# Residual stream with tokens on partitions: norms on one number per token, and tiles turned on TensorE, in a two-layer hybrid decoder step

## What is computed

```python
def rms_norm(x, g):
    y = x * rsqrt(mean(x * x, axis=-1) + EPS)
    return y * g
...
for l in range(2):
    h = rms_norm(x, norm_mix_pre[l])
    m = even_mixer(h) if l == 0 else odd_mixer(h)      # gating MLP + short conv | retention
    x = x + rms_norm(m, norm_mix_post[l])
    h = rms_norm(x, norm_x_pre[l])
    x = x + rms_norm(cross_attn(l, h, mem_k[l], mem_v[l]), norm_x_post[l])
    h = rms_norm(x, norm_ffn_pre[l])
    x = x + rms_norm(ffn(l, h), norm_ffn_post[l])
```

## Time and profile before

| | |
|---|---|
| median of 3 runs | 1286.12 us (1285.82 to 1286.32) |
| the profiled execution | 1280.77 us, of it the span 1278.7 us |
| PE busy | 1176.1 us (92% of the span) |
| DVE busy | 766.4 us (60%) |
| ACT busy | 584.6 us (46%) |
| POOL busy | 296.8 us (23%) |
| mean clock granted to PE | 0.974 of full |
| read from and written to HBM | 233.6 MB, 182 GB/s |

### The profile page before, as it was taken

How to read it: one execution, slowest core, us unless ns; L and a number is a source line. 1 busy time by engine, 2 the same in 40 slices (tenths; PEclk the granted TensorE clock), 3 DMA queues, 4 the chain that set the end, 5 groups by cost and what they waited for, 6 DMA issues and landing times.

```text
span 1278.7 us, 22925 instructions
## 1 busy us (share of the span) xinstructions
PE 1176.1 (92%) x8557; PEld 1085.2 (85%) x8557; DVE 766.4 (60%) x1020; ACT 584.6 (46%) x940; POOL 296.8 (23%) x521
## 2 busy tenths in 40 slices
PE   6999999997999999799999888899999979999995
PEld 4999898696999999699999333798986869999994
DVE  3685835427888743676555677457345278888343
ACT  5446543435666544523345221256334356665432
POOL 5001201114555620200000111004002135646202
PEclk9999999998999999899999899899999989999998
DMA  9748475832545445445444799847848325554531
GB/s 210 233 130 280 152 257 166 301 105 67 180 160 167 133 149 185 156 132 166 156 140 138 254 366 359 279 157 274 278 145 293 128 73 165 164 164 126 170 112 37
DMA packets 177267, 233.64 MB, mean 183 GB/s; under 512 B 5374, under 2 KB 153226, under 8 KB 177200
## 3 DMA queue, kind: packets, MB, share of 16 engines
q1 hardware_dynamic: 159088, 169.09, 40.8%
q0 software_dynamic: 18112, 63.60, 14.5%
HBM read 207.50 MB, written 25.16 MB: 182 GB/s over the span
## 4 chain that ended last, share of the span: by engine, by line
PE 83%; DVE 9%; ACT 5%; issue 2%; DMA 0%; POOL 0%; SPq 0%; ACTq 0%; DVEq 0%
PE ps L392 68%; PE ps L556 5%; ACT wh L324 2%; DVE xT L472 2%; DVE wl L327 2%; PE ps L1207 1%; PE ps L1308 1%; PE ps L1343 1%; PE ps L1319 1%; DVE rstd L433 1%; PE ps L1241 1%; PE ps L1219 1%; DVE raw L962 1%; PE ps L1292 1%; DVE hl L450 1%
## 5 line engine op out<-in xcount | busy, mean ns | idle before, releaser
L327 DVE TENSOR_TENSOR wl<-raw,wh 128x2048 fp32r<-128x2048 f32 (+2 forms) x154 | 331.7, 2154 | 309.6 <-ACT wh L324 309.5
L392 PE MATMUL ps<-hh,wh 128*128 128x288 f32 x1600 | 483.9, 302 | 34.8 <-DVE hl L450 28.2
L392 PE MATMUL ps<-hl,wh 128*128 128x288 f32 x1600 | 476.6, 298 | 0.0
L392 PE MATMUL ps<-hh,wl 128*128 128x288 f32 x1600 | 475.0, 297 | 0.0
L324 ACT ACTIVATE wh<-raw 128x2048 fp32r<-128x2048 f32 (+3 forms) x154 | 277.7, 1803 | 293.8 <-PE ps L392 292.8
L392 PEld LDWEIGHTS ps<-hh,wh 128*128 128x128 f32 x1600 | 304.1, 190 | 41.5 <-issue 33.7
L392 PEld LDWEIGHTS ps<-hh,wl 128*128 128x128 f32 x1600 | 305.7, 191 | 0.0
L392 PEld LDWEIGHTS ps<-hl,wh 128*128 128x128 f32 x1600 | 305.2, 191 | 0.3
L392 PE MATMUL ps<-aH,wh 128*128 128x288 f32 x352 | 104.2, 296 | 0.0
L392 PE MATMUL ps<-aL,wh 128*128 128x288 f32 x352 | 103.9, 295 | 0.0
L392 PE MATMUL ps<-aH,wl 128*128 128x288 f32 x352 | 103.6, 294 | 0.0
(11 more groups left out here) (296 smaller groups left out, 1642.1 us busy)
## 6 DMA issues: line engine op xcount, KB each, us to landing
raw<-w_ffn_up SPq DMA_DIRECT2D x44, 1024.0 KB, 5.1
raw<-w_in_odd SPq DMA_DIRECT2D x24, 1024.0 KB, 5.2
raw<-state_retention SPq DMA_DIRECT2D x16, 1024.0 KB, 7.4
out<-raw POOLq DMA_DIRECT2D x16, 1024.0 KB, 7.8
ring<-cache_mem_k POOLq DMA_DIRECT2D x14, 1024.0 KB, 5.6
raw<-w_ffn_down SPq DMA_DIRECT2D x16, 768.0 KB, 4.4
raw<-w_in_even SPq DMA_DIRECT2D x10, 1024.0 KB, 6.0
raw<-w_ffn_down SPq DMA_DIRECT2D x16, 640.0 KB, 4.1
```

Source lines behind the costliest of these rows:

```text
L327: e.tensor_tensor(wl[:, c % 2, 0:kn, :], src, wh[:, c % 2, 0:kn, :].bitcast(F32), ALU.subtract).then_inc(lo_ready, 1)
L392: mm = pe.matmul(out, lhsT, rhs, start=(kc == 0 and n_k == 0 and n == 0), stop=(kc == g.nk - 1 and n_k == kn - 1 and n == 2))
```

## The change

The stream is kept as `xn`: three groups of 128 tokens on partitions (tokens 0 to 127, 128 to 255, and 160 to 287, so that the third is full; `TOK`) by 1024 features. There a token's norm is one number on its partition.

- **Behind a branch**: ACT copies output tiles to `mT` already times the gain (DVE takes the last tile). `sums` leaves three tiles of squares; `ssq` uses the squares as weights against one column of ones, three token groups each, so that the sum is three columns of 128 tokens. `root_out` and `invert_out` work on 128 x 3. A throw-away root of one number loads ACT's table earlier. `turn_out` turns the four feature tiles of each half and token group to token rows (24 transposes), and `add_piece` on DVE adds them times the token's number into `xn`, in nine pieces of 256, 256 and 512 columns (`SPANS`) by three groups. POOL's `scale_branch` is gone.
- **Before a branch**: `turn_in` turns `xn` back, three transposes for each of eight feature tiles; `high_in` and `low_in` take `hh` and `hl` straight from PSUM. The squares are taken on ACT from `xn` by rows with an accumulated sum (`row_squares`), root and reciprocal are of 128 x 3, and `invert_in` and `spread` bring 1/root back to the transposed layout: a diagonal matrix for each group, multiplied with ones.
- **Where**: at the three direct places (`xo` to `up` twice, `down` to `in_odd`) as one sequence (`joint_act`, `joint_dve`, `joint_tokens`, a new `first_step`), whose second chunk begins with the passes that need only the high half (`late`). Under `xk` and `xv` the turns are hooks after single chunks. The transposes of old conv tails move from behind `xo` to between its chunks.
- **Start and end**: `xn` is loaded as it is (96 prompt rows twice) and stored by SP from `xn` at the end; `xT`, `yn` and their copies are gone.

The diff, cut:

```diff
-        def invert(dve, n):
-            dve.wait_ge(root_ready, n + 1)
-            dve.reciprocal(rstd[:], root[:]).then_inc(rstd_ready, 1)
...
+        def sums(dve, q):
+            dve.wait_ge(sq_ready, CREDIT + 8 * q + 4)
+            dve.tensor_tensor(sq[:, 0:2, :], sq[:, 0:2, :], sq[:, 2:4, :], ALU.add).then_inc(sum_step, 1)
...
+            dve.tensor_tensor(sq[:, 0, :], sq[:, 0, :], sq[:, 1, :], ALU.add).then_inc(sum_step, 1)
+
+        def ssq(pe, q):
+            pe.wait_ge(sum_step, 3 * q + 3)
+            for t in (0, 6, 7):
+                pe.wait_ge(sq_ready, CREDIT + 8 * q + t + 1)
+                for g in range(3):
+                    mm = pe.matmul(ps[:, 7, g:g + 1], sq[:, t, TOK[g]:TOK[g] + P], ones[:, 0:1], start=t == 0 and g == 0, stop=t == 7,
+                                   skip_group_check=True)
...
+        def root_out(act, q):
+            act.wait_ge(ssq_ready, q + 1)
+            act.activation(root_out_col, ps[:, 7, 0:3], ACT.Sqrt, bias=eps_col, scale=1.0 / D).then_inc(root_ready, 1)
...
+        def add_piece(dve, q, n):
+            span, g = divmod(n, 3)
+            c0, c1 = SPANS[span]
+            half = c0 // 512
+            dve.wait_ge(m_nat, 6 * q + 3 * half + g + 1)
+            dve.scalar_tensor_tensor(out=xn[:, g, c0:c1], in0=ps[:, NAT[half][g], c0 - 512 * half:c1 - 512 * half],
+                                     scalar=small[:, 67 + g:68 + g], in1=xn[:, g, c0:c1], op0=ALU.mult,
+                                     op1=ALU.add).then_inc(x_ready, 1)
...
+        def turn_in(pe, q, k, bank):
+            span = next(n for n, (c0, c1) in enumerate(SPANS) if k * P < c1)
+            if k >= 4:
+                pe.wait_ge(h_lo, DT * q + k - 3)
+            for g in range(3):
+                if q:
+                    pe.wait_ge(x_ready, pieces_done(q - 1, 3 * span + g + 1))
+                tr = transpose(pe, ps[:, bank, TOK[g]:TOK[g] + P], xn[:, g, k * P:(k + 1) * P])
...
+        def spread(pe, q):
+            pe.wait_ge(diag_ready, q + 1)
+            pe.wait_ge(h_lo, DT * q + DT)
+            for g in range(3):
+                mm = pe.matmul(ps[:, BN, TOK[g]:TOK[g] + P], ones[:], diag[:, g, :], start=True, stop=True)
...
+        def joint_act(act, g, q):
+            root_out(act, q)
+            held(act, g, True)
+            for k in range(DT):
+                high_in(act, q + 1, k, JOINT_BANKS[k % 4])
+            for r in range(3):
+                row_squares(act, q + 1, r)
+            root_in(act, q + 1)
...
+            for half in range(2):
+                cut = slice(512 * half, 512 * half + 512)
+                sp.wait_ge(x_ready, pieces_done(3 * DEPTH - 1, 3 * half + 2))
+                sp.dma_start(y_prompt[0].rearrange("(r p) d -> p r d", p=P)[:, :, cut], xn[:, 0:2, cut]).then_inc(s("y_stored"), 16)
```

More of the change, by code:

```diff
@@ L357, in held, with trio @@
             split(e, *target(g, g.steps - 1, g.per - 1, True), high)
+        def trio(pe, g, pairs, half, j, c, r0, k, passes):
+            xh, xl = pairs(r0 + k)
+            w_h = wh[:, c % 2, k, j * P:(j + 1) * P]
+            w_l = wl[:, c % 2, k, j * P:(j + 1) * P]
+            three = ((w_h, xh), (w_h, xl), (w_l, xh))
+            for n in passes:
+                mm = pe.matmul(ps[:, 2 * half + j, 0:T], three[n][0], three[n][1], start=k == 0 and n == 0,
+                               stop=k == DT - 1 and n == 2)
+            return mm
         def products(pe, g, pairs, freed, base, natural=False, i0=0, i1=None, turn=0,
-                     hook=None, need=None):
+                     hook=None, need=None, after=0, late=False, between=None):
             i1 = g.steps if i1 is None else i1
             def step(i):
-                for idx in range(g.per):
+                for idx in range(after, g.per):
                     half, kc = divmod(idx, g.nk)
@@ L460, in add_branch @@
[L460 to L484 removed]
+        NAT = ((4, 5, 6), (7, 4, 5))
@@ L1726, in step @@
                             dve.tensor_tensor(zb[:, t, :, 2:PAD], groups(ps[:, t, 0:T]), groups(rstd[:]), ALU.mult).then_inc(s("up_taken"), 1)
-                        split(dve, *target(gu, i, half, last), False)
+                        if not (first and half == 0):
+                            split(dve, *target(gu, i, half, last), False)
                         for t, tile in pair:
```

510 lines of the change are left out of this document (304 added, 206 removed).

## The result

The changed kernel takes **1252.82 us** in the median (1248.29, 1251.33 and 1254.31; a fourth run of 1477.54 us at a mean granted clock of 0.747 was disturbed: it counts in this median, which would be 1251.33 without it, and not in the ratio), the kernel before 1286.22 us. The ratio is 0.9727 with a 95% interval of 0.9697 to 0.9757: 2.7% faster. The profiled execution has 1248.29 us, its span 1246.6.

A forecast was written before the change was run, and what follows sets the result against it. TensorE, busy 92% of the span, was taken as the bound, standing still at three joints. Gains 2 x 6.7 + 7.8 + 0.4 + 10.2 = 31.8 us gave 1249.0 or 1254.3, rounded up to 1255; range 1248 to 1268.

The forecast's parts named there:

- Joint after attention: Attention's output product to up, twice: products start sooner after the branch; gain 7.5 us, 6.7 with the moved conv-tail transposes.
- P: The last product of a branch, from which all sums start; 289.05 us at the joint after attention.
- the gap and the clock behind it: Old joint after attention: PE stands still, the clock falls to 0.50; 22.95 us for 6.4 of matmuls, 16.5 lost.
- Odd joint: Down to the odd input: weight split comes ahead of the rotations, fourth chunk begins at 548.6, not 556.5; gain 7.8 us.
- Covered boundaries: Two boundaries under the memory's key and value products: some 7 us of PE work gone, 7.3 new; gain 0.2 each.
- End: After the last product: adds end at P+5.9, span closes 5.9 us after the store's issue; gain 10.2, 2 either way.
- Start: Program start: extra load, copies of `xT` gone, 24 transposes among products; counted 0, between 2 us gain and 2 loss.
- the squares may reach the spread late by 1.4: At the start, the squares (3.8 us and a table load) may delay the spread of 1/root by 1.4 us.
- The clock held at the joints: Its rival: the clock still falls at the joints, costing 3.0 us, 1.8 at the odd one; 1262 us, chance 0.27.
- Starving: Covered boundaries: three of DVE's weight splits late by 2.39 us each, 7.2 in all; 1261 to 1262 us, chance 0.12.
- One-column products at 0.48: Five boundaries: nine one-column products cost 3.1 us more at each, at 0.48 apiece; 1270 us, chance 0.06.
- Store closes sooner: End: hardware queue closes 2 us sooner; its case also has the odd joint saving its last wait; 1251 us, chance 0.14.

The follow-up runs named there:

- The fillers: Kernel before, with throw-away transposes or ones-products on TensorE in the three joints' gaps: 1284.63 us with transposes, 1284.38 with products, against 1285.32.
- the two omissions: Kernel before, without GpSimd's scaling of seven tiles (1264.45 us), or with the reciprocal behind a branch on 3 columns, not 288 (1272.50); both together 1260.03.
- the kernel without the root: Changed kernel without the throw-away root behind each branch that loads ACT's table early: 1251.05 us in one run.

## Why the prediction was right, and where it was not

The time came out 2.2 us under the forecast of 1255 (3.7 for the 1251.33 above), and by the profiled executions the sum was 31.8 for 32.1. But it agreed in part by luck, because errors cancelled. The medians of ten and five later executions (1285.47 and 1251.01) differ by 34.5: the profiled execution of before, at 1280.77, was among its fastest, and the 2.4 us between 34.5 and 32.1 stand in no term and were not followed.

- **Joint after attention, right to half a us, on a path that it had read well.** Forecast from P: products +6.5, second chunk +14.95, third +21.8. Measured +7.13, +15.31, +22.37 (0.13 of each is that I count from the last product's start here, and counted from 289.05 there). The one-column products are what was mis-sized: 108 instructions took 12.5 us, so 54 products 0.23 each and not 0.14 (they are two instructions each, as all fp32 products here), and nine of them hold PE until +2.2. The old end was read 0.15 late (the third chunk's first product stands at 318.25, not 312.0 + 6.4), and the new one came 0.44 late. Gain 6.96 less 0.84 for the tails: 6.0 and 5.8 in the table for 6.7.
- **What the old joint lost was misread.** The text put 16.5 us down to the gap and the clock behind it. The fillers showed that the clock was 1.1 us of it where they held it, and the two omissions that DVE was the price: slow beside GpSimd, and held by the long reciprocal. The gain did not depend on the wrong reading, since both ends of it were taken from rows. A reader who had followed it would have filled the gap and won 1.1 us at one joint and nothing in the time.
- **Odd joint**, 7.8 for 8.1 at the fourth chunk (+38.13 to +30.07), less the 0.9 of the split in `down`, which the sum did not have.
- **Covered boundaries**, 0.2 forecast, 1.3 and 1.7 measured: 1.1 and 1.3 of it from the 14th to the 23rd chunk and their like in layer 1, the rest in attention, not followed. Counted in layer 0 from each PE instruction's start to the next one's, the new work took 7.4 us for 7.3 (one-column products 1.9, 48 transposes 4.9, spread 0.6). What went away was counted low, 8.5 for 7: the old sums were 4.5 and not 3.9, and the key and value products take 4.0 less, of which 3.0 was PE's wait for `wl`, now gone.
- **End**, 10.2 for 12.0. Two errors of opposite sign: adds that end 7.7 behind the last product and not 5.9, and the store, closed 2.5 us behind its issue, not 5.9. Of the first, 1.3 is the token's number, ready at 3.1 and not 1.8 (nine one-column products in 2.1 us, behind a wait of 0.3), and the rest mostly the adds, 0.75 each and not 0.66 behind transposes at half clock. Where the clock held, in the kernel without the root, they took 0.67 and the span ended at +10.47, so that fall cost 0.2. The prediction named the second as open by 2 us; it was 3.4.
- **Start**, 0 forecast with 2 either way, 3.1 measured. The step that failed is "the squares may reach the spread late by 1.4": they did (1.93), and the third chunk's weight split stood behind them on ACT as well, which the text left out: +2.54 together. Another 0.52 comes at the fifth chunk, not followed. The slow transposes at the start of the kernel before, which the prediction read as no higher clock, are no evidence on it: the profile's granted clock is 1.00 there (9 to 11 us), and why they took 0.29 each is open.
- **Cases.** The clock held at the joints of the profiled execution; in two of the other profiles it fell at the odd one, for 1.4 us. Starving (0.12) did not come. One-column products at 0.48 did not come, 0.23 did. "Store closes sooner" was the better half of the third case.

The odd layer's mixer, which the change doesn't touch, took 1.5 us less: the retention stage, where the clock falls and comes back several times, had one fall fewer. It took 3.75 more in the run without the root. That is why the whole times of single runs say little about steps of one us, and why all of them are read here at aligned products.

## What to carry to other kernels

When PE stands still and its clock falls, ask first who keeps it waiting: fill the gap in a copy of the kernel, look whether the clock was really held, and if the time stays, the clock was a symptom. Look at the same instruction's duration with and without GpSimd running beside it before you split elementwise work between DVE and GpSimd; turning the layout so that a norm is one number per partition paid here because it took that shared work away, more than for its short reciprocal. An early table load is only worth something if ACT would otherwise be last: here it sat beside PE's products anyway, and put early it delayed a weight split.

## What was not expected of the hardware

- DVE, 128 x 288, both inputs in SBUF: 1.04 us while GpSimd multiplied, 0.51 in the next microsecond without it. With one input in PSUM: 0.45 us beside GpSimd and without it.
- Transposes of fp32 hold TensorE's full clock (1.00 in 296:298, with nothing else on PE) as well as products with ones do. At the end of the program nine one-column products and 24 transposes without a pause kept it in three profiles of the changed kernel and its variants (2.82 us for the transposes in the one without the root) and lost it in four (4.47). What decides stays open.
- A one-column fp32 product costs 0.23 us, against 0.48 for 288 columns.
- The same last stores close 2.5 us behind SyncE's issue and 5.9 behind GpSimd's, 3.95 us of the program's end with the dearer issue.
